# Pairing each 64-slot expert with a 128-slot expert, block by block, in a two-layer decoder trunk

## The chip, the cores and the metric

The kernel runs on one core of a Trainium2 chip. The metric is device time in microseconds. The kernel before takes 1368.06 us (median of 3 runs, 1367.66 to 1368.17).

## What is computed

256 tokens of width 1024 go through two decoder layers in float32. The part that matters here is the channel mixer of the second layer, eight experts of which each token uses two:

```
logits = xn @ w_router                      # (256, 8)
top_v, top_i = top_k(logits, 2);  gates = softmax(top_v) put at top_i
for e in range(8):
    ye = (silu(xn @ w_gate[e]) * (xn @ w_up[e])) @ w_down[e]    # 1024 -> 3584 -> 1024
    out = out + gates[:, e:e+1] * ye
```

Around it stand an attention layer with its dense mixer, a pooling mixer, norms and a gated per-layer input. They are the same in both kernels.

## The kernel before

**Precision.** Each float32 weight is used as a high part and a low part in a 32-bit matmul type. ScalarE copies the raw weights to `w_hi` (`split_hi`, L297), VectorE subtracts to get `w_lo` (`split_lo`, L314), and TensorE runs three matmuls per product: high by high, low by high, high by low (`product`, L334 to L336).

**Units.** Weights come in units of 128x2048 elements (1 MB), numbered `u` in one sequence over the whole kernel. SP loads them into seven buffers `raw`; a load waits for the `split_lo` of the unit seven before it. `w_hi` and `w_lo` have three buffers each (`SPLIT = 3`): `split_hi(u)` waits until TensorE has used unit u-3 (`unit_used`). Both splits run two units ahead in the order of the code (`AHEAD = 2`).

**Experts.** The tokens of an expert are gathered into 128 slots by a matmul with a 0/1 matrix (`pick`), and the result is scattered back by a matmul with its transpose (`pick_t`). An expert's turn has seven blocks of 512 hidden columns. A block has six units: two of the gate matrix (G1, G2 here), two of the up matrix (U1, U2) and two of the down matrix (D1, D2) for the hidden columns of the block before. Between them ScalarE does the silu (L1386), VectorE the product `hiddens` (L1887), TensorE turns the hidden tile (L865), and ScalarE and VectorE split it again (`hidden_hi`, `hidden_lo`).

**Small experts.** VectorE sorts the experts by their token count (`sort_experts`, `place_experts`, in turn 0). The three with the fewest tokens have 64 slots: their rows are put side by side as high and low part, so that up and down products take two matmuls and not three (`product_few`, L1048 and L1049). Hidden tiles are turned and summed by a matmul with `fold` (L862). Expert 0 runs first while the sort is done, then the three small ones, then four of 128 slots:

```
turn(1, 0, few=True)
turn(2, 0, few=True, few_before=True)
turn(1, 2, few=True, few_before=True)
turn(2, 2, few_before=True)
with pe.Fori(3, pairs + 1) as it:      # one pass, two turns
    ...
turn(1, turns - 1, end=True)
```

**Between turns.** Every second turn gathers the tokens of the two next experts in its last block, in banks 5 and 6 (`gather_pair`). The result of a turn is complete in banks 3 and 4 after the first block of the next; ScalarE and VectorE split it (`result_hi` L1503, `result_lo` L2121), TensorE scatters it in four quarters in the second block, and VectorE adds each, times its gate, to the residual (`add_result`, L2130). TensorE, ScalarE, VectorE and SP each run a list of instructions in the order written in the code, and wait for each other by semaphores.

Of the kernel before, what the change touches and what calls it, by code (L numbers as in the profile page):

```python
# [20 lines left out]
F32 = mybir.dt.float32  # L21
# [46 lines left out]
RANK_AT = (0, 5, 6, 7, 1, 2, 3, 4)  # L68
FEW_AT = (1, 2, 3)


def trunk(nc, dram):
    ctx = ExitStack()
    with ctx:
# [66 lines left out]
        gate_at = sb("gate_at", [P, TT, 2 * NE])  # L141
        place_at = sb("place_at", [P, TT, 2 * NE + 1])
        rank_at = sb("rank_at", [P, NE])
# [3 lines left out]
        order = sb("order", [P, NE], I32)  # L147
# [19 lines left out]
        few_hidden = h_t_hi[:, :].rearrange("p (c h s) -> p c h s", c=4, h=2)  # L167
        sort_cols, sort_area = qk_gain[:, :, :].rearrange("p a d -> p (a d)"), rope[:, :, :, :].rearrange("p t a n -> p (t a n)")
        sort_key, sort_rank, sort_over, sort_count = (sort_cols[:, n * NE:(n + 1) * NE] for n in range(4))
        sort_own = sort_cols[:, DH:DH + NE * NE].rearrange("p (a e) -> p a e", a=NE)  # L170
        sort_work = sort_area.rearrange("p (t a e) -> p t a e", t=TT, a=NE)
# [149 lines left out]
        def load(eng, u, view, k=0):  # L321

            dst = raw_slot(u).rearrange("p (c n) -> p c n", c=view.shape[1])
            if in_wide(u):
                eng.dma_start(dst, view).then_inc(extra_landed[u - U_WIDE], 16)
                return
            if u >= RAW:
                before_it = ring(u) - RAW
                split_wait(eng, before_it if before_it < U_WIDE else before_it + EXTRA, k)
            eng.dma_start(dst, view).then_inc(landed[ring(u) % RAW], 16)  # L330
# [21 lines left out]
        def _(sp):  # L352
# [81 lines left out]
            def expert_units(e, e_before, u, first=False):  # L434

                units = []
                for f in range(FB):
                    views = [expert_rows(w, e, 4 * half, 4, 512 * f, 512) for w in (ge, ue) for half in range(2)]
                    if f or not first:
                        views += [expert_rows(de, e if f else e_before, 4 * ((f - 1) % FB) + 2 * half, 2, 0, D)  # L440
                                  for half in range(2)]
                    units += [(u + n, view) for n, view in enumerate(views)]
                    u += len(views)
                return units

            def load_expert(e, e_before, k):
                for u, view in expert_units(e, e_before, U_TURN):
                    load(sp, u, view, k)


            first_expert = expert_units(0, None, U_MOE, first=True)
# [15 lines left out]
            e_before = 0  # L467
            for at in range(1, NE):
                e = expert_at(slice(at, at + 1))
                load_expert(e, e_before, at - 1)  # L470
                e_before = e
            extra = sp.value_load(more[0:1, 0:1], min_val=0, max_val=NE)
            with sp.If(extra > 0):
                load_expert(0, expert_at(slice(NE - 1, NE)), NE - 1)
                with sp.Fori(1, NE) as it:
                    load_expert(expert_at(bass.ds(it, 1)), expert_at(bass.ds(it - 1, 1)), it + (NE - 1))
            turns = extra + (NE - 1)
            e = expert_at(slice(NE - 1, NE))
            for half in range(2):
                load(sp, U_TURN + half, expert_rows(de, e, 4 * (FB - 1) + 2 * half, 2, 0, D), turns)  # L480
# [40 lines left out]

        def gathered_of(i, e):

            return ps[:, 5 + i % 2, :].rearrange("p (c e s) -> p c e s", c=2, e=2)[:, :, e, :]
# [43 lines left out]
        def _(pe):  # L568
# [441 lines left out]
            def gather_pair(part, t0, k=0):  # L1010

                if part == 0:
                    pe.wait_ge(pick_ready, t0 + 3 + k)
                    if t0:
                        pe.wait_ge(added, 4 * (t0 + k))
                    else:
                        pe.wait_ge(rows_split_lo, 2)
                else:
                    pe.wait_ge(xe_lo_ready, 2 * (t0 + 1 + k) + 2)
                for c in range(4 * part, 4 * part + 4):  # L1020
                    for rows, tt in ((a_hi, 0), (a_hi, 1), (a_lo, 0), (a_lo, 1)):
                        at = (c % 2) * 2 * SLOTS
                        last = nc.tensor.matmul(ps[:, 5 + (c % 4) // 2, at:at + 2 * SLOTS],  # L1023
# [3 lines left out]
                    if c % 2:  # L1027
                        last.then_inc(gathered, 1)

            def scatter(q, t, k=0):  # L1030

                pe.wait_ge(y_lo_ready, t + 1 + k)
                pe.wait_ge(pick_t_copied, t + 1 + k)
                if q < 2 and t % 2 == 0:
                    pe.wait_ge(xe_lo_ready, 2 * (t + 3 + k))
                elif q < 2:
                    pe.wait_ge(added, 4 * (t + k))
                else:
                    pe.wait_ge(added, 4 * (t + k) + q - 1)
                tt, half = q // 2, q % 2  # L1040
                for y, stop in ((y_hi, False), (y_lo, True)):
                    last = nc.tensor.matmul(ps[:, 5 + q % 2, :], pick_t[:, tt * P:(tt + 1) * P],  # L1042
# [8 lines left out]
            def down(u, f, half, g, k=0, end=False, h_t=(h_t_hi, h_t_lo), few=False):  # L1051
# [3 lines left out]
                for n in range(2):  # L1055
                    for c in range(2):
                        at = (2 * half + c) * P
                        first, stop = f == 0 and half == 0 and c == 0, f == FB - 1 and half == 1 and c == 1
                        w = weights(u, c, 512 * n, 512, D)
                        if few:  # L1060
                            last = product_few(ps[:, 3 + n, :], h_t_hi[:, at:at + P], w, first, stop)
                        else:
                            last = product(ps[:, 3 + n, :], (h_t[0][:, at:at + P], h_t[1][:, at:at + P]), w, first, stop)
# [4 lines left out]
            def turn(t0, k=0, end=False, few=False, few_before=False):  # L1068

                x = xb if t0 == 2 else xe  # L1070

                def x_of(c):
                    return x[:, 2 * c * P:(2 * c + 1) * P], x[:, (2 * c + 1) * P:(2 * c + 2) * P]

                for f in range(FB):
                    u, g = turn_unit(t0, f), JF + FB * t0 + f
                    for n, freed in ((0, silu_ready), (1, hidden_ready)):
                        for half in range(2):
                            unit(u, k)
                            if f == 0 and n == 0 and t0 < 2:  # L1080
                                pe.wait_ge(xe_lo_ready, 2 * (t0 + k) + (half + 1) * (t0 + 1))
                            if half == 0:
                                pe.wait_ge(freed, g + FB * k)
                            for c in range(4):
                                d, w = 4 * half + c, weights(u, c, 0, 512, 512)
                                if few and n == 1:
                                    both = x[:, 2 * d * P + FEW:2 * d * P + FEW + P]
                                    last = product_few(ps[:, n, :], both, w, d == 0, d == KD - 1)
                                else:
                                    last = product(ps[:, n, :], x_of(d), w, d == 0, d == KD - 1)  # L1090
                            last.then_inc(unit_used, 1)
                            u += 1
                        if t0 == 0 and f == 1 and n == 0:
                            transpose_hidden(g - 1, k)
                    if f == 1 and t0:
                        scatter(0, t0 - 1, k)
                        scatter(1, t0 - 1, k)
                    if f == 2:
                        if t0:
                            pe.wait_ge(pick_t_copied, t0 + k)  # L1100
                        for tt in range(TT):
                            last = nc.tensor.transpose(ps[:, 7, tt * P:(tt + 1) * P],
                                                       pick_of(t0 // 2, tt).bitcast(F32), ident[:, :])
                        last.then_inc(pick_transposed, 1)
                    if f or t0:
                        if f == 1 and t0:
                            pe.wait_ge(y_lo_ready, t0 + k)
                        for half in range(2):
                            if f == FB - 1 and t0 != 1:
                                gather_pair(half, t0, k)  # L1110
                            down(u, (f - 1) % FB, half, g - 1, k, few=few if f else few_before)
                            if end and f == FB - 1 and half == 0:
                                transpose_hidden(g, k)
                            u += 1
                    if f == 1 and t0:
                        scatter(2, t0 - 1, k)
                        scatter(3, t0 - 1, k)
                    if (f or t0) and not (end and f == FB - 1):
                        transpose_hidden(g, k, few)
# [3 lines left out]
            turn(0)  # L1123
            pe.wait_ge(more_ready, 1)
            extra = pe.value_load(more[0:1, 0:1], min_val=0, max_val=NE)
            turns = extra + (NE - 1)
            pairs = pe.value_load(more[0:1, 1:2], min_val=0, max_val=NE // 2) + (NE // 2 - 1)
# [1270 lines left out]
```

## Time and profile before

| quantity | value |
|---|---|
| median of 3 runs | 1368.06 us |
| the profiled execution | 1368.13 us |
| its span | 1366.4 us |
| TensorE busy | 1325.6 us, 97% |
| VectorE busy | 1154.0 us, 84% |
| ScalarE busy | 951.8 us, 70% |
| granted TensorE clock, all slices | full |
| bytes read from HBM | 420.27 MB |

The shares are over the whole span. Matmuls are pipelined: the profile gives each a length of 0.39 us, while one starts every 0.23 us, so that a TensorE share near 100% still can hold short waits. The seven turns after the first take the stretch from 492 to 1322 us.

### The profile page before, as it was taken

To read this page: it belongs to the slowest core of one execution; us is meant where nothing else is said; L and a number is where in the kernel's file an instruction comes from. 1 tells how busy PE (TensorE), PEld (TensorE's weight loads), DVE (VectorE), ACT (ScalarE), POOL (GpSimd) and SP (SyncE) were. 2 spreads that over 40 slices of the span, in tenths; PEclk is the share of its full clock that TensorE was granted. 3 is DMA by queue.
4 is the path that set the end of the run, shared out by engine and by line. 5 is a ranking of instruction groups with operands and counts; after the bars stand their busy time and mean duration, and the time that the engine had idled before them with its cause. 6 is when DMAs were issued, how large, how long until landed. Compare 5 with 4: busy or idle time off the path is not lost.

```text
span 1366.4 us, 17261 instructions
## 1 busy us (share of the span) xinstructions
PE 1325.6 (97%) x6404; PEld 1082.8 (79%) x6404; DVE 1154.0 (84%) x970; ACT 951.8 (70%) x874; POOL 71.5 (5%) x110
## 2 busy tenths in 40 slices
PE   8999999999999999999999999999999999999998
PEld 7776888888877887777777777888888888888887
DVE  6897655556889989999999999998898899889886
ACT  5676544446777777777777777777777777776775
POOL 2120910000200000000000000000000000000000
PEclk9999999999999999999999999999999999999999
DMA  8743765555299889999999999999999999999980
GB/s 305 266 130 89 256 203 195 185 185 162 86 357 347 317 323 359 393 395 393 394 393 390 380 394 395 394 372 371 337 351 375 377 349 359 376 337 359 358 329 31
DMA packets 197860, 422.46 MB, mean 309 GB/s; under 512 B 13064, under 2 KB 37392, under 8 KB 197776
## 3 DMA queue, kind: packets, MB, share of 16 engines
q1 hardware_dynamic: 197776, 421.35, 85.2%
q8 instruction: 52, 0.85, 0.3%
q14 instruction: 32, 0.26, 0.0%
HBM read 420.27 MB, written 1.05 MB: 308 GB/s over the span
## 4 chain that ended last, share of the span: by engine, by line
PE 74%; DVE 16%; ACT 5%; issue 3%; SPq 1%; DMA 1%; POOL 0%; ACTq 0%; DVEq 0%; POOLq 0%
PE ps L334 19%; PE ps L336 19%; PE ps L335 19%; DVE w_lo L314 12%; PE ps L885 5%; ACT w_hi L297 4%; PE ps L883 3%; PE ps L1048 1%; PE ps L865 1%; PE ps L1023 1%; PE ps L1049 1%; PE ps L862 1%; PE ps L882 1%; DMA raw<-in_attn_w_qkv_dram 1%; PE ps L1042 1%
## 5 line engine op out<-in xcount | busy, mean ns | idle before, releaser
L314 DVE TENSOR_TENSOR w_lo<-raw,w_hi 128x2048 fp32r<-128x2048 f32 x382 | 867.8, 2290 | 128.6 <-ACT w_hi L297 127.4
L297 ACT ACTIVATE w_hi<-raw 128x2048 fp32r<-128x2048 f32 x385 | 732.6, 1914 | 122.2 <-PE ps L336 100.0
L334 PE MATMUL ps<-w_hi,xe 128*128 128x512 f32 x448 | 178.4, 398 | 3.0 <-DVE w_lo L314 2.9
L336 PE MATMUL ps<-w_hi,xe 128*128 128x512 f32 x448 | 174.8, 390 | 0.0
L335 PE MATMUL ps<-w_lo,xe 128*128 128x512 f32 x448 | 174.5, 390 | 0.0
L334 PE MATMUL ps<-w_hi,h_t_hi 128*128 128x512 f32 x360 | 141.4, 393 | 0.5 <-DVE w_lo L314 0.5
L336 PE MATMUL ps<-w_hi,h_t_lo 128*128 128x512 f32 x360 | 140.3, 390 | 0.0
L335 PE MATMUL ps<-w_lo,h_t_hi 128*128 128x512 f32 x360 | 140.2, 389 | 0.0
L334 PE MATMUL ps<-w_hi,xb 128*128 128x512 f32 x280 | 111.4, 398 | 1.9 <-DVE w_lo L314 1.9
L885 PE MATMUL ps<-a_all,w_hi 128*128 128x512 f32 x308 | 109.8, 396 | 0.0
L336 PE MATMUL ps<-w_hi,xb 128*128 128x512 f32 x280 | 109.2, 390 | 0.0
L335 PE MATMUL ps<-w_lo,xb 128*128 128x512 f32 x280 | 109.1, 390 | 0.0
L334 PEld LDWEIGHTS ps<-w_hi,xe 128*128 128x128 f32 x448 | 84.1, 188 | 21.7 <-DVE w_lo L314 5.3
L336 PEld LDWEIGHTS ps<-w_hi,xe 128*128 128x128 f32 x448 | 84.1, 188 | 18.1
L335 PEld LDWEIGHTS ps<-w_lo,xe 128*128 128x128 f32 x448 | 84.2, 188 | 16.4
L883 PE MATMUL ps<-a_all,w_lo 128*128 128x256 f32 x352 | 90.9, 279 | 0.0
L2286 POOL TENSOR_TENSOR rstd<-mean_sq,minus_half 128x1 f32<-128x1 f32 (+2 forms) x20 | 23.9, 1199 | 1267.2 <-DVE mean_sq L1588 1186.0
L334 PE MATMUL ps<-w_hi,a_all 128*128 128x512 f32 (+1 forms) x216 | 84.5, 391 | 0.1
L1048 PE MATMUL ps<-w_hi,h_t_hi 128*128 128x512 f32 x168 | 69.8, 415 | 14.8 <-DVE w_lo L314 13.4
L336 PE MATMUL ps<-w_hi,a_all 128*128 128x512 f32 (+1 forms) x216 | 81.9, 379 | 0.0
L335 PE MATMUL ps<-w_lo,a_all 128*128 128x512 f32 (+1 forms) x216 | 81.6, 378 | 0.0
L334 PEld LDWEIGHTS ps<-w_hi,h_t_hi 128*128 128x128 f32 x360 | 67.6, 188 | 15.6 <-DVE w_lo L314 2.4
(319 smaller groups left out, 1856.9 us busy)
## 6 DMA issues: line engine op xcount, KB each, us to landing
raw<-in_moe_w_gate_dram SPq DMA_DIRECT2D x112, 1024.0 KB, 7.6
raw<-in_moe_w_up_dram SPq DMA_DIRECT2D x111, 1024.0 KB, 7.4
raw<-in_moe_w_down_dram SPq DMA_DIRECT2D x111, 1024.0 KB, 7.4
raw<-in_attn_w_qkv_dram SPq DMA_DIRECT2D x11, 1024.0 KB, 12.6
raw<-in_ffn_w_gate_dram SPq DMA_DIRECT2D x11, 1024.0 KB, 5.3
raw<-in_ffn_w_up_dram SPq DMA_DIRECT2D x11, 1024.0 KB, 5.3
raw<-in_ffn_w_down_dram SPq DMA_DIRECT2D x11, 1024.0 KB, 5.0
raw<-in_ple_w_gate_dram SPq DMA_DIRECT2D x8, 1024.0 KB, 6.9
```

Source lines behind the costliest of these rows:

```text
L297: nc.scalar.activation(w_hi[:, u % SPLIT, :], raw_slot(u), ACT.Copy).then_inc(hi_ready, 1)
L314: nc.vector.tensor_tensor(w_lo[:, u % SPLIT, :], raw_slot(u), w_hi[:, u % SPLIT, :].bitcast(F32), ALU.subtract).then_inc(lo_ready, 1)
L334: nc.tensor.matmul(out, x[0], w[0], start=first, stop=False)
L335: nc.tensor.matmul(out, x[0], w[1], start=False, stop=False)
L336: return nc.tensor.matmul(out, x[1], w[0], start=False, stop=last)
L862: last = nc.tensor.matmul(ps[:, 2, n * FEW:(n + 1) * FEW], hidden[:, n * P:(n + 1) * P], fold[:, :], start=True, stop=True)
L865: last = nc.tensor.transpose(ps[:, 2, n * P:(n + 1) * P], hidden[:, n * P:(n + 1) * P], ident[:, :])
L882: nc.tensor.matmul(ps[:, bank, :], w[0], a_all[:, :, cols], start=True, stop=False)
L883: last = nc.tensor.matmul(ps[:, bank, 0:SEQ], w[1], a_hi[:, cols], start=False, stop=False)
L885: last = nc.tensor.matmul(ps[:, bank, :], w[0], a_all[:, :, cols], start=False, stop=c == KD - 1)
L1048: nc.tensor.matmul(out, x, w[0], start=first, stop=False)
L2286: return nc.gpsimd.tensor_tensor(rstd[:, at:at + n], mean_sq[:, at:at + n], minus_half[:, 0:n], ALU.pow)
```

## The change

The order of the experts by token count becomes (0, 5, 1, 6, 2, 7, 3, 4), so that after expert 0 there are three pairs of a small and a large expert, and one large expert last. A pair runs its 14 blocks alternately: a block of the small one, a block of the large one, and so on. The down units of a block belong to the block of the same expert, two blocks before. Each of the two has its own pair of result banks, `Y_BANKS` (3 and 4, 6 and 7). Scatter and turned picks share bank 5; the gather uses banks 5 and 2. The small hidden tile has its own buffer (`few_t`), and the picks of both experts are turned together and copied by ScalarE instead of VectorE. The hidden tile of one block is turned after the first gate unit of the next. The silu moves behind the third `split_hi` of a block, and `hiddens` behind the fifth `split_lo`. The places of the experts in the sort grow from 8 to 19 (`PLACES`), for turns that only run when an expert has more tokens than slots. `SPLIT`, `RAW` and `AHEAD` stay.

```diff
-RANK_AT = (0, 5, 6, 7, 1, 2, 3, 4)
+RANK_AT = (0, 5, 1, 6, 2, 7, 3, 4)
+PLACES = NE + len(SECOND)
...
+        few_t = p_t_hi[:, 0, :]
+        picks_t = p_t_lo[:, 0, :]
+        Y_BANKS = (6, 3)
...
+        PAIR_BLOCKS = [(f, e) for f in range(FB) for e in range(2)]
+        SCATTERS = {(0, 1, 1): (-1, 0), (0, 1, 3): (-1, 1), (0, 1, 5): (-1, 2), (1, 0, 1): (-1, 3),
+                    (1, 0, 5): (0, 0), (1, 1, 1): (0, 1), (1, 1, 3): (0, 2), (1, 1, 5): (0, 3)}
...
+            def pair(k, first=False):          # TensorE
+                for f, e in PAIR_BLOCKS:
+                    few, x, g = e == 0, (xe, xb)[e], block_at_seq(f, e)
...
+                    for n in range(2):
+                        for half in range(2):
...
+                            gate_or_up(u + 2 * n + half, n, half, x, g, k, few)
+                            if n == 0 and half == 0:
...
+                                transpose_hidden(g - 1, k, few=e == 1)
+                            if f == 3 and e == 0 and n == 1 and half == 0:
+                                transpose_picks(k, 2)
+                            if f == FB - 1 and e == 1 and n == 1:
+                                gather_piece(half, k + 2, g + FB * k)
+                            between(2 * n + half)
...
+                    down(u + 4, f_down, 0, g_down, t_down, k, few=few)
...
+                    down(u + 5, f_down, 1, g_down, t_down, k, few=few)
+                    between(5)
...
+            def pair(k, first=False):          # ScalarE
+                for f, e in PAIR_BLOCKS:
+                    g, u = block_at_seq(f, e), pair_unit(f, e, first)
+                    for n in range(4 if first and f == 0 and e == 0 else 6):
+                        split_hi(u + n + AHEAD, k)
+                        if f == 0 and e == 1 and n == 0 and not first:
+                            result_hi(u - 1, -1, k)
+                        if f == 1 and e == 0 and n == 2:
+                            result_hi(u - 1, 0, k, free=not first)
+                        if n == 1:
+                            hidden_hi(g - 1, k, few=e == 1)
+                        if n == 2:
+                            silus(g, u + 1, k)
...
+            def pair(k, slots, first=False):   # VectorE
+                for f, e in PAIR_BLOCKS:
...
+                        split_lo(u + n + AHEAD, k)
+                        if f == 0 and e == 1 and n == 0 and not first:
+                            result_lo(-1, k)
+                        if f == 1 and e == 0 and n == 2:
+                            result_lo(0, k)
+                        if n == 1:
+                            hidden_lo(g - 1, k, few=e == 1)
+                        if n == (3 if bare else 4):
+                            hiddens(g, u + 3, k)
...
+                        if f == 4 and e == 0 and n == 3:
+                            picks(4, 1, k, iota_slot[:, :])
...
-                    then(nc.vector.tensor_tensor(sort_work, a[:, :, :].unsqueeze(2).to_broadcast([P, TT, NE, NE]),
-                                                 sort_own.unsqueeze(1).to_broadcast([P, TT, NE, NE]), ALU.mult))
+                    then(nc.vector.tensor_tensor(sort_work, a[:, :, :].unsqueeze(2).to_broadcast([P, TT, PLACES, NE]),
+                                                 sort_own.unsqueeze(1).to_broadcast([P, TT, PLACES, NE]), ALU.mult))
...
-            turn(1, 0, few=True)
-            turn(2, 0, few=True, few_before=True)
-            turn(1, 2, few=True, few_before=True)
-            turn(2, 2, few_before=True)
+            pair(0, first=True)
+            pair(2)
             with pe.Fori(3, pairs + 1) as it:
-                turn(1, (it - 1) * 2)
-                turn(2, (it - 1) * 2)
-            turn(1, turns - 1, end=True)
+                pair((it - 1) * 2)
+            last_turn(turns - 1)
```

## Rows read from the trace of the kernel before

**Rows 1.** Busy time by engine in stretches of time: small block, large block, turns, whole stretch.
```profile
core 0: us, PE busy (x) PEld busy (x) DVE busy (x) ACT busy (x) POOL busy (x), PEclk, DMA share, GB/s
578.26:593.82 15.56, 14.43 (x65) 11.23 (x64) 14.34 (x9) 12.04 (x8) 0.00 (x0) 1.00 1.04 394
936.44:953.23 16.79, 16.79 (x85) 14.18 (x84) 14.86 (x10) 11.61 (x10) 0.00 (x0) 1.00 1.03 379
720.70:835.06 114.36, 106.34 (x477) 82.33 (x475) 107.00 (x71) 87.91 (x62) 0.00 (x0) 1.00 1.04 389
1077.30:1197.63 120.33, 120.07 (x551) 99.20 (x550) 108.08 (x67) 87.31 (x59) 0.00 (x0) 1.00 1.00 365
492.46:1321.71 829.25, 807.50 (x3665) 651.30 (x3665) 756.26 (x480) 619.86 (x431) 0.00 (x0) 1.00 1.00 371
```

**Rows 2.** Who waited for whom, small block 578.26 to 593.82 (total, times, longest).
```profile
PEld ps L1048 <- DVE w_lo L314: 2.3, 3, 1.5
DVE w_lo L314 <- ACT w_hi L297: 1.2, 2, 0.9
```

**Rows 3.** VectorE in order of time, small block (start, length, instruction, idle before).
```profile
583.61 2.29 DVE L314 TENSOR_TENSOR w_lo<-raw,w_hi 128x2048 fp32r<-128x2048 f32 x1
586.27 2.29 DVE L314 TENSOR_TENSOR w_lo<-raw,w_hi 128x2048 fp32r<-128x2048 f32 x1 [0.37 <-ACT w_hi L297]
589.41 4.49 DVE L314 TENSOR_TENSOR w_lo<-raw,w_hi 128x2048 fp32r<-128x2048 f32 x2 [0.85 <-ACT w_hi L297]
593.82 0.68 DVE L1887 TENSOR_TENSOR tmp<-tmp,ps 128x512 f32<-128x512 f32 x1
594.42 4.49 DVE L314 TENSOR_TENSOR w_lo<-raw,w_hi 128x2048 fp32r<-128x2048 f32 x2
```

**Rows 4.** ScalarE in order of time, the same block.
```profile
586.97 0.60 ACT L1386 ACTIVATE tmp<-ps 128x512 f32<-128x512 f32 x1 [0.74 <-PE ps L336]
587.47 5.51 ACT L297 ACTIVATE w_hi<-raw 128x2048 fp32r<-128x2048 f32 x3
```

**Rows 5.** TensorE in order of time, the same block: the first matmul of each part.
```profile
581.20 0.50 PE L334 MATMUL ps<-w_hi,xe 128*128 128x512 f32 x1
...
586.77 0.39 PE L1048 MATMUL ps<-w_hi,xe 128*128 128x512 f32 x1
...
588.62 0.50 PE L1048 MATMUL ps<-w_hi,xe 128*128 128x512 f32 x1
...
591.76 0.50 PE L1048 MATMUL ps<-w_hi,h_t_hi 128*128 128x512 f32 x1 [1.04 <-DVE w_lo L314]
...
593.96 0.50 PE L1048 MATMUL ps<-w_hi,h_t_hi 128*128 128x512 f32 x1
...
595.93 1.00 PE L862 MATMUL ps<-fold,tmp 128*128 128x64 f32 x8
596.76 0.50 PE L334 MATMUL ps<-w_hi,xe 128*128 128x512 f32 x1
```

**Rows 6.** TensorE in order of time, between two large blocks.
```profile
923.37 0.60 PE L865 MATMUL ps<-ident,tmp 128*128 128x128 f32 x4
923.72 0.48 PE L334 MATMUL ps<-w_hi,xb 128*128 128x512 f32 x1
```

**Rows 7.** Groups of instructions by line, 492.46 to 1321.71 (busy, mean ns, idle before).
```profile
L2130 DVE SCALAR_TENSOR_TENSOR resid<-ps,gate_at,resid 128x512 f32<-128x512 f32 x28 | 19.6, 743 | 0.0
L2121 DVE TENSOR_TENSOR y_lo<-ps,y_hi 128x1024 fp32r<-128x1024 f32 x7 | 8.5, 1217 | 0.3 <-ACT y_hi L1503 0.3
L1503 ACT ACTIVATE y_hi<-ps 128x1024 fp32r<-128x1024 f32 x7 | 7.2, 1022 | 0.0
```

**Rows 8.** VectorE and TensorE in order of time, sort and placing in turn 0.
```profile
405.14 0.22 DVE L2076 TENSOR_TENSOR rope<-qk_gain 128x64 f32<-128x64 f32 x1
...
421.23 0.28 DVE L2094 TENSOR_TENSOR rope<-place,qk_gain 128x128 f32<-128x128 f32 x1
...
410.81 0.50 PE L334 MATMUL ps<-w_hi,xe 128*128 128x512 f32 x1 [1.55 <-DVE w_lo L314]
...
425.16 0.50 PE L334 MATMUL ps<-w_hi,h_t_hi 128*128 128x512 f32 x1 [0.18 <-DVE w_lo L314]
```

More of the change, by code:

```diff
@@ L1066, in down, with gate_or_up @@
                 last.then_inc(unit_used, 1)
[L1068 to L1073, printed above, removed]
+            def gate_or_up(u, n, half, x, g, k=0, few=False):
+                unit(u, k)
+                if half == 0:
+                    pe.wait_ge((silu_ready, hidden_ready)[n], g + FB * k)
+                for c in range(4):
+                    d, w = 4 * half + c, weights(u, c, 0, 512, 512)
+                    if few and n == 1:
+                        both = x[:, 2 * d * P + FEW:2 * d * P + FEW + P]
+                        last = product_few(ps[:, n, :], both, w, d == 0, d == KD - 1)
+                    else:
+                        rows = x[:, 2 * d * P:(2 * d + 1) * P], x[:, (2 * d + 1) * P:(2 * d + 2) * P]
+                        last = product(ps[:, n, :], rows, w, d == 0, d == KD - 1)
+                last.then_inc(unit_used, 1)
@@ L1075, in turn, with transpose_picks, first_turn @@
+            def transpose_picks(k, experts):
+                pe.wait_ge(added, 4 + 4 * k)
+                for e in range(experts):
+                    for tt in range(TT):
+                        at = (e * TT + tt) * P
+                        last = nc.tensor.transpose(ps[:, 5, at:at + P], pick_of(e, tt).bitcast(F32), ident[:, :])
+                last.then_inc(pick_transposed, experts)
+            def first_turn():
                 for f in range(FB):
-                    u, g = turn_unit(t0, f), JF + FB * t0 + f
@@ L1077, in turn @@
-                    for n, freed in ((0, silu_ready), (1, hidden_ready)):
+                    u, g = turn_unit(0, f), JF + f
+                    gather = f == FB - 1
+                    for n in range(2):
                         for half in range(2):
[L1079 to L1094, printed above, removed]
@@ L1115, in turn @@
[L1115 to L1119, printed above, removed]
+                    if f:
+                        down(u + 4, f - 1, 0, g - 1, 0)
+                        if gather:
+                            gather_piece(2, 0, g)
+                            gather_piece(3, 0, g)
+                        down(u + 5, f - 1, 1, g - 1, 0)
+                        if not gather:
+                            transpose_hidden(g)
@@ new lines, in piece_hi, with result_hi @@
+            def piece_hi(i, k):
+                act.wait_ge(gathered, 3 + i + 2 * k)
+                for e, x in enumerate((xe_parts, xb_parts)):
+                    last = nc.scalar.activation(x[:, 2 * i:2 * i + 2, 0, :], gathered_of(i, e), ACT.Copy)
+                last.then_inc(xe_hi_ready, 1)
+            def result_hi(u, t, k=0, free=True):
+                used(u, k)
+                if free:
+                    act.wait_ge(scattered, 4 * t + 4 * k)
+                nc.scalar.activation(y_hi[:, :].rearrange("p (b n) -> p b n", b=2), y_of(t), ACT.Copy).then_inc(y_hi_ready, 1)
@@ new lines, in last_turn @@
+            def last_turn(k):
+                for f in range(FB):
+                    g, u = JF + FB + f, last_unit(f)
+                    for n in range(6 if f else 8):
+                        split_hi(u + n + AHEAD, k)
+                        if f == 0 and n == 6:
+                            result_hi(u + 5, -1, k)
+                        if f == 2 and n == 2:
+                            result_hi(last_unit(0) + 7, 0, k)
+                        if n == 1:
+                            hidden_hi(g - 1, k)
+                        if n == 2:
+                            silus(g, u + 1, k)
+                        if f == 4 and n == 3:
+                            act.wait_ge(scattered, 4 + 4 * k)
+                            copy_picks(2 + k, slice(0, TT * P), 1)
+                        if f == FB - 1 and n == 4:
+                            hidden_hi(g, k, to=a_hi[:, 0:512])
@@ L1534, in _ @@
                 nc.scalar.activation(a_hi[:, tt * D:(tt + 1) * D], xs[:, tt, :], ACT.Copy).then_inc(rows_split_hi, 1)
-            turn(0)
+            first_turn()
             act.wait_ge(more_ready, 1)
-            extra = act.value_load(more[0:1, 0:1], min_val=0, max_val=NE)
+            extra = act.value_load(more[0:1, 0:1], min_val=0, max_val=EXTRA_TURNS)
             turns = extra + (NE - 1)
-            pairs = act.value_load(more[0:1, 1:2], min_val=0, max_val=NE // 2) + (NE // 2 - 1)
-            turn(1, 0, few=True)
-            turn(2, 0, few=True)
-            turn(1, 2, few=True)
-            turn(2, 2)
+            pairs = act.value_load(more[0:1, 1:2], min_val=0, max_val=EXTRA_TURNS // 2) + 3
+            pair(0, first=True)
+            pair(2)
             with act.Fori(3, pairs + 1) as it:
-                turn(1, (it - 1) * 2)
-                turn(2, (it - 1) * 2)
-            turn(1, turns - 1, end=True)
+                pair((it - 1) * 2)
+            last_turn(turns - 1)
             split_hi(U_TURN + AHEAD, turns)
@@ L2203, in _ @@
-            turn(0, few_next=(True, True))
+                    u, g = turn_unit(0, f), JF + f
+                    for n in range(0 if f else 1, 4):
+                        split_lo(u + n + AHEAD)
+                        if f == 1 and n == 1:
+                            hidden_lo(g - 1)
+                        if f == 1 and n == 3:
+                            sort_experts()
+                        if f == 2 and n == 2:
+                            place_experts()
+                        if f in (3, 4) and n == 2:
+                            rows_lo_of(f - 3)
@@ new lines, in last_turn @@
+            def last_turn(k):
+                for f in range(FB):
+                    g, u = JF + FB + f, last_unit(f)
+                    for n in range(6 if f else 8):
+                        split_lo(u + n + AHEAD, k)
+                        if f == 0 and n == 6:
+                            result_lo(-1, k)
+                        if f == 2 and n == 2:
+                            result_lo(0, k)
+                        if n == 1:
+                            hidden_lo(g - 1, k)
+                        if n == (3 if f == FB - 1 else 4):
+                            hiddens(g, u + 3, k)
+                        if (f, n) in LAST_SCATTERS:
+                            t, q = LAST_SCATTERS[f, n]
+                            add_result(q, t, k)
+                        if f == FB - 1 and n == 4:
+                            hidden_lo(g, k, to=(a_hi[:, 0:512], a_lo[:, 0:512]))
@@ L2204, in _ @@
+            first_turn()
             dve.wait_ge(more_ready, 1)
[L2205 removed]
+            extra = dve.value_load(more[0:1, 0:1], min_val=0, max_val=EXTRA_TURNS)
             turns = extra + (NE - 1)
[L2207 to L2211 removed]
+            pairs = dve.value_load(more[0:1, 1:2], min_val=0, max_val=EXTRA_TURNS // 2) + 3
@@ L2212, in _ @@
+            pair(0, iota_few[:, :], first=True)
+            pair(2, iota_few[:, :])
             with dve.Fori(3, pairs + 1) as it:
-                turn(1, (it - 1) * 2)
-                turn(2, (it - 1) * 2)
-            turn(1, turns - 1, end=True)
+                pair((it - 1) * 2, iota_next)
+            last_turn(turns - 1)
             split_lo(U_TURN + AHEAD, turns)
```

462 lines of the change are left out of this document (274 added, 188 removed).

## The prediction

> **What bounds the kernel now.** I read the stretches of time first, block by block, because the share of TensorE over the whole span says only that it is rarely idle. The turns of the experts take 829.25 us of the span. A block of a large expert takes 16.79 us with TensorE busy all the time and VectorE 14.86. A block of a small expert takes 15.56, with TensorE at 14.43 and VectorE at 14.34 [rows 1]. So large blocks are bound by TensorE, and small ones by something that neither engine's busy time shows.
>
> The waits of a small block name it: TensorE waits for `w_lo` three times, and VectorE waits for `w_hi` twice in the same block [rows 2]. The order of time shows the loop. TensorE starts U1 at 586.77, when G2 is done. Only then may ScalarE split D1, which takes G2's buffer. It does the silu first at 586.97, then D1's high part at 587.47; VectorE follows at 589.41, after an idle 0.85, and TensorE starts D1 at 591.76 [rows 3 to 5]. From there VectorE runs without a gap: D1, D2, `hiddens`, and the next G1 from 594.42, which TensorE takes up at 596.76.
>
> What is lost: from U1 to the next G1 are 9.99 us [rows 5]. Work in it is 4 short units of 8 matmuls. A matmul starts every 0.2265 us: from 581.20 to 586.77 there are 24, the first of them 0.11 longer after its wait (5.57 = 24 x 0.2265 + 0.13) [rows 5]. That makes 7.25, and fold takes 596.76 - 595.93 = 0.83. So 9.99 - 8.08 = 1.91 us are lost in each of 21 small blocks, 40 us in all. That is all that interleaving could win.
>
> **The steady pair of blocks.** TensorE's work is unchanged: the same matmuls, turns and folds in another order. The question is whether the 1.91 goes. A split buffer is free only when TensorE is done with the unit three before. At the end of G2 of a small block VectorE has already waited 0.37 and 0.85 for it [rows 3], so the buffers were full, and TensorE was two units behind them. A large block ahead can't make them fuller: VectorE's spare time there is spent waiting for a free buffer. Four short units follow as before. I therefore walk the new order with the same distances, counted from U1's start:
> - ScalarE begins D1's high part at +0.20 (586.97 - 586.77), as the silu now stands behind it. VectorE starts 1.94 later (589.41 - 587.47), at +2.14, and TensorE 2.35 after that (591.76 - 589.41), at +4.49. Before it was +4.99 [rows 3 to 5].
> - D1's high part takes a further 1.83 in a run (5.51 for three), then the silu 0.50, so D2's high part starts at +2.53 and VectorE at +4.47. It was free at +4.34 (splits in a run are 2.20 apart, 4.49 - 2.29) [rows 3, 4]. TensorE has D2 at +6.82.
> - The next unit is G1 of the large block. `hiddens` no longer stands ahead of it, so VectorE begins at +6.67 and TensorE has it at +9.02.
>
> Work in this stretch is 7.25 alone, since fold has moved into the large block. Lost: 9.02 - 7.25 = 1.77. So silu and `hiddens`, 0.50 and 0.60, leave the chain, but fold's 0.83 no longer covers it.
>
> The pair then is: small block 5.44 for the gate, 0.49 for turning the large hidden tile (a large block's 16.79 less 72 x 0.2265 = 16.31; the turns themselves fill 0.35 of it [rows 1, 6]), and 9.02, together 14.95. Large block: 16.31 + 0.83 + 0.11 for the start after a wait + 0.11 after the fold = 17.36. Sum 32.31, against 15.56 + 16.79 = 32.35 now. Over 21 pairs of blocks: -1 us. Bounds: -40 if no wait is left, and +8 if both gate starts and D2 slip by a further 0.2 each (21 x 0.4).
>
> **Between turns.** The same four gathers, 28 scatters and 16 turned picks. A small turn costs 114.36 against 7 x 15.56 = 108.92 [rows 1], 5.4 with its gather, part of it in time that was lost anyway. A large one without a gather costs 120.33 - 7 x 16.79 = 2.8. In a pair, the small expert's block 1 has `result_hi` between D1 and the silu and `result_lo` between D1 and D2. The chain gets later by VectorE's 1.22 less its wait of 0.13, so some 1.0; two scatter quarters of 2 x 0.2265 = 0.45 in the same block cover 0.9 of it. The `picks` ahead of a G1 cost at most 0.35 (the nearest row, a VectorE pass of 128 elements, takes 0.28 [rows 8]). The other results fall into large blocks with spare time. I take +0.5 for three pairs. Bounds: nothing to gain beyond the -1.8 of one scatter set hidden in lost time, and +11 from the rival below [rows 7].
>
> **Sort and placing.** They stand in VectorE's queue in turn 0, where TensorE already waits for `w_lo` behind them: 1.55 at 410.81, and 0.18 at 425.16 [rows 8]. So every longer instruction counts in full. An operation on 64 elements takes 0.22 and one on 128 takes 0.28, about 0.001 per element. Four placing operations go from 128 to 304 elements: 4 x 0.18 = 0.7. Three sort operations go from 64 to 152: 0.3. New are a compare, two operations for `iota_next` and a wait that was not there, less one copy: 0.2 + 0.6 + 0.1 - 0.2 = 0.7. Together +1.7; bounds 0 (the large block absorbs it in its spare 1.9, 16.79 - 14.86 [rows 1]) and +3. The memsets added on GpSimd come long before anyone waits and cost nothing. The copy of the picks, now on ScalarE, lies in a large block once and once in D2's stretch, after the low split of D1: nothing.
>
> **Transfers.** Small turns move 394 GB/s now, and no wait for a landing shows on ScalarE [rows 1, 2]. Interleaved, 12 MB-units take 32.3 us, 12 x 1.0486 / 32.3 = 390 GB/s. It was hidden at the higher rate, so it stays hidden; without that cover the wait would fall on ScalarE ahead of each high split.
>
> **The sum.** -1.0 + 0.5 + 1.7 = +1.2 us on the profiled execution's 1368.13, hence 1369.3; this execution stands 0.07 above the median, so 1369.2 for the median.
>
> The trace has the two regimes that the Trainium skill's page Perfetto Trace Analysis (Optimization Strategy) speaks of: where the most-contended engine changes over time, interleaving the regimes may help. By that rule the wait would go and the time would be near 1330; it is rival A. The same section says that a gap repeating on the engine that should be saturated can mean too few buffers for the next tile. The gap before D1 repeats in each small block, and by this second rule interleaving alone leaves it. The chain of rows 3 to 5 bears out the second.
>
> **Rivals.**
> - A. Interleaving evens the load out in full: VectorE goes into a small block far enough ahead. For it: averaged over two blocks, VectorE needs 29.2 and TensorE 30.5 of 32.35. Against it: three split buffers. Price -40 + 0.5 + 1.7, hence 1330. Chance 5%.
> - B. Only the first wait stays, 4.49 - 3.63 = 0.86, and D2 and the next G1 come without one, because ScalarE and VectorE have shorter queues there than I count. It saves (1.77 - 0.86) x 21 = 19 us more: 1350. Chance 12%.
> - C. Slower: the between-turn work of a pair lands one for one in the short stretch of a small block, since nothing is spare there. Place: block 1 of the small expert and the blocks of `picks`. Price per pair: 1.02 + 1.22 + 2 x 0.74 + 0.35 = 4.1 [rows 7], 12 over three, less the 0.5 counted: 1381. It decides once ScalarE waits for `scattered` or VectorE for a scatter ahead of D1 or D2, as bank 5 now serves all four quarters in turn. Chance 12%.
> - D. The pairs don't run as described, because more tokens than slots ask for extra turns. The rooms by rank are the same, so this would show in both. Chance under 1%.
>
> **How the numbers follow.** My forecast has 70%, with some 2.5 us to both sides. The time of this kernel can be told from no change beyond about 0.2%, 2.7 us: below 1365.3 is faster, above 1370.8 slower. Faster: A and B 0.17, and 0.06 of the forecast's share, together 0.22. Slower: C 0.12 and a quarter of the forecast's share, 0.29. Same: 0.49. The range 1360 to 1376 holds the forecast with some slip in the D chain on both sides (0.2 to 0.4 per small block is 4 to 8 us), and leaves out A, B and most of C.
>
> **What would show it.** In a pair, one `hiddens` to the second next should be 32.3 apart. TensorE should wait for `w_lo` at D1 (0.9), D2 (0.4) and at G1 of the large block (0.3), and nowhere in the large block. ScalarE's idle time before the high split should be released by TensorE in both kinds of block. The wait at 410.81 should grow by 0.5 and that at 425.16 by 1.2. I am wrong if the wait before D1 is gone, or if TensorE waits inside large blocks.

## The result

The changed kernel takes 1371.39 us (median of 13 runs, 1369.88 to 1373.38), the kernel before 1368.21 us (13 runs, 1367.66 to 1370.13). The ratio is 1.0019, with a 95% interval of 1.0011 to 1.0028: some 2.6 us slower, at the edge of what can be told from no change. 1369.2 had been forecast, in a range of 1360 to 1376.

The profiled execution of the changed kernel has a span of 1368.6 us against 1366.4. TensorE executes 6404 matmuls in both and is busy 97% of both spans. Nearly all of the difference stands in one place. Turn 0, from its first product of the hidden tile to its last, goes from 99.21 to 101.08. The 49 blocks after it go from 829.25 [rows 1] to 829.46. What comes before and after is the same within 0.2.

Stretches of time of the changed kernel (columns as in rows 1): a small block, the large block after it, all 49 blocks, and turn 0.
```profile
661.49:677.35 15.86, 14.92 (x66) 11.39 (x64) 14.77 (x10) 12.72 (x9) 0.00 (x0) 1.00 1.03 381
677.35:693.87 16.52, 16.43 (x77) 13.69 (x77) 14.49 (x9) 11.78 (x8) 0.00 (x0) 1.00 1.02 380
494.47:1323.93 829.46, 804.74 (x3666) 650.64 (x3665) 756.52 (x472) 619.60 (x435) 0.00 (x0) 1.00 1.01 373
393.39:494.47 101.08, 97.28 (x442) 78.96 (x441) 92.30 (x76) 70.22 (x49) 0.00 (x0) 1.00 0.94 340
```
The same turn of the kernel before:
```profile
393.25:492.46 99.21, 97.25 (x442) 78.95 (x441) 90.89 (x75) 70.03 (x48) 0.00 (x0) 1.00 0.97 347
```
A pair of blocks takes 15.86 + 16.52 = 32.38, where one of each took 15.56 + 16.79 = 32.35 [rows 1]. VectorE is busy 1.4 us longer in turn 0, and TensorE as long as before: its wait grew.

TensorE in order of time in one small block of a pair: the first matmul of U1, D1, D2 and of G1 of the large block. They answer to rows 5.
```profile
668.44 0.39 PE L1111 MATMUL ps<-w_hi,xe 128*128 128x512 f32 x1
...
673.00 0.50 PE L1111 MATMUL ps<-w_hi,p_t_hi 128*128 128x512 f32 x1 [0.77 <-DVE w_lo L324]
...
675.28 0.50 PE L1111 MATMUL ps<-w_hi,p_t_hi 128*128 128x512 f32 x1 [0.17 <-DVE w_lo L324]
...
677.49 0.50 PE L344 MATMUL ps<-w_hi,xb 128*128 128x512 f32 x1
```
Counted from U1's start, D1 comes at 4.56, D2 at 6.84 and G1 at 9.05. The walk had 4.49, 6.82 and 9.02. All three delays are there, though the profile marks only two of them as waits (0.77 and 0.17): eight matmuls take 1.81, and G1 comes 2.21 after D2, so 0.4 late. TensorE is busy 16.43 of the large block's 16.52.

### The profile page after: what moved, and what is told of

It reads as the page before. It is cut to its first block, busy times and chain, and to the rows that moved or that the text cites. A ratio compares the mean times of both kernels' runs of the same rounds, so it can differ in the third digit from the quotient of the medians.

```text
span 1368.6 us, 17326 instructions
## 1 busy us (share of the span) xinstructions
PE 1323.0 (97%) x6404; PEld 1082.3 (79%) x6404; DVE 1155.5 (84%) x963; ACT 951.6 (70%) x879; POOL 72.3 (5%) x133
## 4 chain that ended last, share of the span: by engine, by line
PE 76%; DVE 15%; ACT 5%; issue 2%; SPq 1%; DMA 1%; POOL 0%; ACTq 0%; DVEq 0%; POOLq 0%
PE ps L344 20%; PE ps L346 19%; PE ps L345 19%; DVE w_lo L324 11%; PE ps L952 5%; ACT w_hi L307 4%; PE ps L950 3%; PE ps L929 1%; PE ps L1092 1%; PE ps L932 1%; PE ps L1105 1%; PE ps L949 1%; PE ps L1111 1%; DMA raw<-in_attn_w_qkv_dram 1%; PE ps L1112 1%
## 5 line engine op out<-in xcount | busy, mean ns | idle before, releaser
L344 PE MATMUL ps<-w_hi,xe 128*128 128x512 f32 x392 | 156.3, 399 | 1.7 <-DVE w_lo L324 1.5
L346 PE MATMUL ps<-w_hi,xe 128*128 128x512 f32 x392 | 153.1, 391 | 0.0
L345 PE MATMUL ps<-w_lo,xe 128*128 128x512 f32 x392 | 152.8, 390 | 0.0
L344 PE MATMUL ps<-w_hi,h_t_hi 128*128 128x512 f32 x360 | 141.0, 392 | 2.2 <-DVE w_lo L324 2.2
L344 PE MATMUL ps<-w_hi,xb 128*128 128x512 f32 x336 | 135.2, 402 | 4.1 <-DVE w_lo L324 3.5
L346 PE MATMUL ps<-w_hi,xb 128*128 128x512 f32 x336 | 131.3, 391 | 0.0
L345 PE MATMUL ps<-w_lo,xb 128*128 128x512 f32 x336 | 131.0, 390 | 0.0
L1111 PE MATMUL ps<-w_hi,p_t_hi 128*128 128x512 f32 x168 | 70.3, 418 | 20.0 <-DVE w_lo L324 19.1
L344 PEld LDWEIGHTS ps<-w_hi,xe 128*128 128x128 f32 x392 | 73.7, 188 | 16.7 <-DVE w_lo L324 2.6
L346 PEld LDWEIGHTS ps<-w_hi,xe 128*128 128x128 f32 x392 | 73.6, 188 | 15.9
L345 PEld LDWEIGHTS ps<-w_lo,xe 128*128 128x128 f32 x392 | 73.8, 188 | 14.3
L344 PEld LDWEIGHTS ps<-w_hi,xb 128*128 128x128 f32 x336 | 63.1, 188 | 23.7 <-DVE w_lo L324 7.8
```

Of the source, the lines that this page charges most:

```text
L344: nc.tensor.matmul(out, x[0], w[0], start=first, stop=False)
L345: nc.tensor.matmul(out, x[0], w[1], start=False, stop=False)
L346: return nc.tensor.matmul(out, x[1], w[0], start=False, stop=last)
L1111: nc.tensor.matmul(out, x, w[0], start=first, stop=False)
```

## The experiments

Each is compared with the kernel before on the same chip.

| kernel | median us | ratio to before, 95% | one small + one large block |
|---|---|---|---|
| turns (before) | 1368.2 | 1 | 15.56 + 16.79 |
| pairs (the change) | 1371.39 | 1.0019 (1.0011 to 1.0028) | 32.38 |
| pairs, silu and `hiddens` at old places | 1389.81 | 1.0153 (1.0137 to 1.0168) | 33.29 |
| pairs, short sort | 1368.58 | 1.0001 (0.9992 to 1.0010) | 32.38 |
| turns, silu late | 1361.49 | 0.9953 (0.9936 to 0.9970) | 15.22 + 16.79 |
| turns, four buffers | 1368.68 | 1.0001 (0.9992 to 1.0010) | 15.56 + 16.79 |
| turns, four buffers, silu late | 1361.68 | 0.9947 (0.9932 to 0.9962) | 14.17 once, later 15.9, + 16.79 |
| the same, half the down bytes | 1344.57 | 0.9826 (0.9810 to 0.9843) | 14.16 + 16.79 |
| pairs, four buffers | 1334.48 | 0.9752 (0.9737 to 0.9767) | 14.14 + 16.47 |
| pairs, fourth buffer for high parts alone | 1336.29 | 0.9762 (0.9747 to 0.9777) | 14.57 + 16.05 |
| pairs, four buffers, half the down bytes | 1333.82 | 0.9748 (0.9733 to 0.9763) | 14.15 + 16.51 |
| pairs, four buffers, short sort | 1334.10 | 0.9746 (0.9733 to 0.9759) | 14.14 + 16.47 |

### Pairs with four split buffers

From the first pair on the split buffers form a ring of four; the fourth ones lie where `xs` and `extra_raw` were.

```diff
+        def slot(u, k):
...
+            return (u - U_TURN) % 4
...
+        def hi_slot(u, k=0):
...
+            at = slot(u, k)
+            return hi_fourth[:, :] if at == 3 else w_hi[:, at, :]
...
+        def lo_slot(u, k=0):
...
+            at = slot(u, k)
+            return lo_fourth[:, :] if at == 3 else w_lo[:, at, :]
...
-                nc.scalar.wait_ge(unit_used, u - SPLIT + 1 + PER_EXPERT * k)
+                nc.scalar.wait_ge(unit_used, u - depth(u, k) + 1 + PER_EXPERT * k)
```

> The changed kernel with a fourth buffer for the high and for the low parts from the first pair on (a split waits for the unit four before, not three; the order of every queue stays). Theory (the three split buffers hold the wait): D1's high part no longer waits for the end of G2, the waits before D1, D2 and the next G1 go, and a pair of blocks falls from 32.4 us to the TensorE work of about 30.6, 21 times: 1333 to 1338 us. If the transfers bind then (12 units in 30.6 us are 411 GB/s, above the 394 of the small turns), it ends later, 1338 to 1350. Rival (ScalarE and VectorE are too slow in the four short units whatever the buffers): within 3 us of 1371.

1334.48 us, 37 less than the three-buffer pairs. A pair of blocks takes 14.14 + 16.47 = 30.61; TensorE's work alone is 32.35 - 1.91 = 30.44 by the numbers of the kernel before. The whole answer to who waited for whom in most of a small block (575.5 to 588):
```profile
ACT p_t_hi L1559 <- PE ps L960: 1.2, 1, 1.2
ACT hi_fourth L337 <- PE ps L376: 0.8, 1, 0.8
ACT tmp L1554 <- PE ps L376: 0.6, 1, 0.6
ACT w_hi L337 <- PE ps L376: 0.4, 1, 0.4
```
TensorE and VectorE are in no line: neither waits. All that is left is ScalarE waiting for TensorE. Over the whole block one wait of 0.2 us of TensorE's weight load for `w_lo` is added. VectorE is busy from end to end of this block, and so is TensorE by the profile; its row, with the large one after it:
```profile
574.59:588.73 14.14, 14.14 (x68) 11.73 (x67) 14.14 (x10) 11.10 (x8) 0.00 (x0) 1.00 1.04 391
588.73:605.20 16.47, 16.47 (x78) 13.67 (x77) 14.85 (x10) 13.34 (x11) 0.00 (x0) 1.00 1.04 395
```
The three buffers held the wait.

### Turns with four split buffers

The same edit in the kernel before.

> The kernel before with the same fourth buffers from turn 1 on. Theory: here the silu stands ahead of D1's high part in ScalarE's queue and itself waits for the end of G2, so that the fourth buffer is of no use to D1, and small blocks stay at 15.5 to 15.6 us: 1367 to 1369 us. Rival (the fourth buffer alone is what counts, pairs or not): 10 to 40 us faster.

1368.68 us, and small blocks at 15.56. ScalarE in order of time there:
```profile
599.84 1.90 ACT L327 ACTIVATE hi_fourth<-raw 128x2048 fp32r<-128x2048 f32 x1
603.34 0.60 ACT L1419 ACTIVATE tmp<-ps 128x512 f32<-128x512 f32 x1 [1.59 <-PE ps L366]
603.84 5.51 ACT L327 ACTIVATE w_hi<-raw 128x2048 fp32r<-128x2048 f32 x3
```
The silu waits 1.59 us for the end of G2, and D1's high part stands behind it in the queue, though its buffer is free. So a deeper ring needs the silu out of its way in ScalarE's queue.

### Pairs with the silu and `hiddens` at their old places

```diff
+                        if n == 2:
+                            silus(g, u + 1, k)
                         split_hi(u + n + AHEAD, k)
...
-                        if n == 2:
-                            silus(g, u + 1, k)
...
-                        if n == (3 if bare else 4):
+                        if n == 3:
                             hiddens(g, u + 3, k)
```

> The changed kernel with the silu again ahead of the third high split of a block, and the product of the hidden tile again ahead of the next block's first low split. Theory (the walk along the chain): D1 gets 0.50 later, the next G1 another 0.6, so that 2.7 us are lost per small block instead of 1.8: 20 us slower than the changed kernel, 1389 to 1393, a pair of blocks at 33.3. Rival (the chain is held by TensorE's release of buffers alone): within 3 us of 1371.

1389.81 us, a pair of blocks at 33.29. Counted from U1's start, D1 comes at 4.98, D2 at 7.18 and G1 at 9.98, nearly where the kernel before had D1 and G1 (4.99 and 9.99). The silu moves D1 by 0.42 and the product adds 0.59 between D2 and G1, against 0.50 and 0.60 in the walk, so both are on the chain. In the changed kernel their new places pay for what fold no longer covers.

### Turns with the silu late

```diff
-                    silus(g, u + 1, k)
                     split_hi(u + 2 + AHEAD, k)
+                    silus(g, u + 1, k)
                     split_hi(u + 3 + AHEAD, k)
```

> The kernel before with one change, the silu behind the third high split of a block; three split buffers. Theory (the walk): D1 comes 0.50 earlier in each small block and D2 at most 0.13 later than VectorE allows, so that 0.3 to 0.5 of the 1.91 us goes: small blocks at 15.05 to 15.25, 6 to 10 us faster, 1358 to 1362. Rival (VectorE's run from D1 to the next G1 starts later for another reason): 1368.

1361.49 us, small blocks at 15.22 instead of 15.56. One line moved is worth 6.4 us to the kernel before by the ratio. In the profiled execution turn 0, which has the line too, went to 97.2, 2.0 less, and the 49 blocks got 5.0 shorter. The steady small blocks, 0.34 each, promise 7.1. Transfers are the likely reason for the rest, though no run tests it: ScalarE waits 7.7 us for landings in these blocks, where it waited for none before.

### Pairs with the sort on 8 places

```diff
-                    then(nc.vector.tensor_tensor(sort_work, a[:, :, :].unsqueeze(2).to_broadcast([P, TT, PLACES, NE]),
-                                                 sort_own.unsqueeze(1).to_broadcast([P, TT, PLACES, NE]), ALU.mult))
+                    then(nc.vector.tensor_tensor(sort_work[:, :, 0:NE], a[:, :, :].unsqueeze(2).to_broadcast([P, TT, NE, NE]),
+                                                 sort_own[:, 0:NE].unsqueeze(1).to_broadcast([P, TT, NE, NE]), ALU.mult))
...
-                pair((it - 1) * 2, iota_next)
+                pair((it - 1) * 2, iota_slot[:, :])
```

The sort itself is cut in the same way, and the subtraction of `base_at` and the two operations for `iota_next` are left out.

> The changed kernel with the sort and the placing on 8 places as before, not 19, and without the two operations that choose the slots of later pairs (turns that only an overfull expert needs are left unprepared). Theory: the 1.9 us that turn 0 got longer come from these operations, and all of them go: 1.5 to 2 us faster than the changed kernel, the stretch from the first to the seventh product of turn 0 back to 99.2 us. Rival (turn 0 is longer because of the copies of the picks on ScalarE or the gather in pieces): under 0.5 us.

1368.58 us, level with the kernel before, and 0.18% below the change by the two ratios. VectorE's part of it, the placing and the low split behind it, in the changed kernel:
```profile
421.86 0.47 DVE L2276 TENSOR_TENSOR tmp<-place,tmp 128x304 f32<-128x304 f32 x1
...
424.83 2.29 DVE L324 TENSOR_TENSOR w_lo<-raw,w_hi 128x2048 fp32r<-128x2048 f32 x1
```
and in the short one:
```profile
422.45 0.28 DVE L2277 TENSOR_TENSOR tmp<-place,tmp 128x128 f32<-128x128 f32 x1
...
423.74 2.29 DVE L324 TENSOR_TENSOR w_lo<-raw,w_hi 128x2048 fp32r<-128x2048 f32 x1
```
Placing takes 424.83 - 421.86 = 2.97 in one and 1.29 in the other, 1.68 less. Yet the profiled turn 0 fell only from 101.08 to 100.70, not to the 99.2 expected. The row of the stretch right behind the sort says why, first in the changed kernel, then in the short one:
```profile
410.50:414.50 4.00, 3.05 (x13) 2.55 (x14) 4.00 (x4) 1.84 (x2) 0.00 (x0) 1.00 0.58 188
```
```profile
410.50:414.50 4.00, 4.00 (x11) 3.15 (x12) 4.00 (x3) 0.85 (x1) 0.00 (x0) 0.57 0.80 254
```
In that execution the granted clock fell to near the lower of its two levels (1.2 of 2.4 GHz) after TensorE's two waits of turn 0. From 410.83 to 413.82 matmuls started 0.43 apart and not 0.23, and nine of them took 3.75 us instead of 2.17, 1.6 more. The same fall stands in the trace of the turns with four buffers, whose turn 0 has the code of the kernel before; it takes 100.78 there, where the kernel before took 99.21:
```profile
392.48:493.26 100.78, 98.86 (x442) 80.08 (x441) 90.87 (x75) 69.99 (x48) 0.00 (x0) 0.98 0.95 342
```
The mean granted clock of most executions is on record, so the two causes can be told apart. Of the changed kernel's 13 executions, the six at a mean clock of 1.000 took 1369.88 to 1370.64 and the seven at 0.998 or 0.999 took 1371.39 to 1373.38. For the kernel before, 37 executions beside the experiments have it: 26 at 1.000 with a median of 1368.14 and none above 1368.68, and 11 below 1.000 with a median of 1369.60. At 1.000 the changed kernel stands at 1370.28, and with the short sort at 1368.27 (six of 11 executions). So the longer sort costs 2.0 us, in every execution, as expected, and the fall of the clock 1.5 in some.

### Four buffers and silu late, turns one after the other

Both edits above in the kernel before.

> The kernel before (turns one after the other) with the fourth split buffers and the silu moved behind D1's high part, as the pairs have it. It asks what the interleaving itself is worth once D1 need not wait. Theory: a small block is then bound by VectorE's 6 x 2.20 + 0.60 + 0.34 = 14.1 us, large blocks stay at 16.8 by TensorE: small blocks from 15.56 to 14.2 to 14.5, in all 1345 to 1350 us. The pairs with four buffers, at 1334.5, would then owe 10 to 15 us to the interleaving. Rival (buffers and the silu's place do it all, interleaving nothing): as fast as the pairs with four buffers, 1334 to 1337.

1361.68 us: missed, 12 us above the band. One early small block did take 14.17, but the next took 15.28 and later ones 15.9. Two of them:
```profile
559.57:573.74 14.17, 14.07 (x65) 11.32 (x64) 14.17 (x9) 10.62 (x8) 0.00 (x0) 1.00 1.04 394
620.86:636.75 15.89, 15.11 (x67) 11.99 (x68) 15.44 (x10) 13.13 (x10) 0.00 (x0) 1.00 1.04 393
```
and the two longest of ScalarE's waits in the second:
```profile
ACT w_hi L327 <- DMA raw<-in_moe_w_gate_dram: 2.4, 3, 0.8
...
ACT w_hi L327 <- DMA raw<-in_moe_w_down_dram: 0.8, 2, 0.6
```
ScalarE waits for landings, which it did nowhere in the 49 blocks of the kernel before. TensorE's weight loads wait 2.4 us for low parts behind it. A block reads 6 x 1.0486 = 6.29 MB; at 394 GB/s that is 15.97 us. The steady small blocks of the kernel before, at 15.56 us, asked for 404 GB/s, already above this rate, but a small turn as a whole (44.0 MB in 114.36 us) only for 385. Here the first blocks outrun the transfers, as far as the seven raw buffers carry, and then the transfers set the pace. The 49 blocks take 824.3, no less than with the silu late alone: what the fourth buffer frees, the transfers take.

### The same with half of the bytes of the down units

```diff
+            if u >= U_TURN and view.shape[1] == 2:
+                dst, view = dst[:, :, 0:512], view[:, :, 0:512]
             eng.dma_start(dst, view).then_inc(landed[ring(u) % RAW], 16)
```

> Turns one after the other, fourth split buffers, silu late, and half of the bytes of each down unit loaded from turn 1 on (the output isn't the reference's). In the run with all bytes, small blocks began at 14.17 us and then went to 15.9, with 394 GB/s flat and ScalarE waiting for landings. Theory (394 GB/s is what transfers give, 6.29 MB then take 15.95 us, and interleaving wins by spreading the bytes over the large blocks): small blocks stay at 14.2, about 17 of them times 1.75, 1330 to 1337 us, level with the pairs. Rival (VectorE's or TensorE's own work keeps them there): 1355 to 1362.

1344.57 us: steady small blocks stay at 14.16, 17 us less in all. That is the transfers' share, and no wait for a landing is left. The forecast of 1330 to 1337 was missed by 8 us. It counted 17 stretched blocks of 1.75 us. Block by block, twelve small blocks got shorter, eight of them by 1.7 us or more, 18.2 us in all. The kernel stays ten us above the pairs, which transfers don't explain.

### Pairs with four buffers: three more

> Pairs with four split buffers, with half of the bytes of each down unit loaded from the first pair on (the second half of the columns is left from an earlier unit, so the output isn't the reference's). It asks whether transfers bind the pairs with four buffers, where ScalarE waited some 27 us for landings. Theory (transfers take a part of the steady time, mostly at the ends of a stretch without boundary work): 2 to 6 us faster than 1334.5, and no waits for landings. Rival (those waits are ahead of need): within 1 us of 1334.5.

1333.82 us, 0.7 less than with all bytes. The waits for landings are gone, but the 2 to 6 us are not gained: those waits lay ahead of need, as the rival has it, and transfers hardly bind the pairs. They are close to it, though: with all bytes the 49 blocks move 391 GB/s on average.

> Pairs with a fourth buffer for the high parts alone; the low parts keep three, and VectorE itself waits for the unit three before. It asks whether the whole chain or only its ScalarE part must start early. Theory: with the high part ready, VectorE can begin D1 at 0.2 us after the end of G2 and TensorE has it at 2.6, a us ahead of its need at 3.6: within 1.5 us of the 1334.5 of both buffers. Rival (VectorE needs the buffer as much): 1345 or more.

```diff
+            if depth(u, k) == 4:
+                nc.vector.wait_ge(unit_used, u - SPLIT + 1 + PER_EXPERT * k)
...
         def lo_slot(u, k=0):
-            at = slot(u, k)
-            return lo_fourth[:, :] if at == 3 else w_lo[:, at, :]
+            return w_lo[:, u % SPLIT, :]
```
1336.29 us, 1.8 above both buffers and so 0.3 outside the band, with intervals that overlap. Nearly all of the gain needs 8 KB per partition, for the high part.

> Pairs with four split buffers and the sort on 8 places: the two findings together. Theory: turn 0 gives back its 1.9 us in full: 1332.5 to 1333. Rival (the stretch after it is now bound by transfers at 394 GB/s, which go on through turn 0 as well, so that the time won is spent waiting for a landing): 1334 to 1334.5.

1334.10 us. The intervals of this and of the long sort overlap, and the clock fell behind the sort in its profiled execution too (0.64 from 410.5 to 414.5). The transfers didn't take the time back there: ScalarE waits for no landing in turn 0, and the 49 blocks take 792.5 against 792.4 with the long sort. The one execution at a mean clock of 1.000 took 1332.75, inside the forecast, and the four at 0.999 took 1334.09 to 1334.48. That speaks for the clock and against the rival, on a single execution. Of the kernels that load all bytes this one is the fastest, by a margin too small to tell from the next.

## Why the prediction was right

- **No gain from interleaving with three buffers: right.** The steady pair was forecast at 32.31 against 32.35 and measured at 32.38. Each of the three steps of the chain came within 0.07. The fourth buffer shows that the ring was the cause, and the old places show that silu and `hiddens` have nearly the cost the walk gave them (0.42 and 0.59 against 0.50 and 0.60).
- **Between turns: right in size, in part by luck.** -1.0 + 0.5 were forecast for the 49 blocks and +0.2 was measured. The steady pairs gave +0.6 (21 x 0.03) and not -1.0, the work between turns -0.4 and not +0.5; the two errors have opposite signs.
- **Sort and placing: right, +1.7 forecast, +1.87 in turn 0.** 0.5 and 1.2 were expected at two waits. The end of the first came 0.5 later against the start of turn 0 (411.45 - 393.39 against 410.81 - 393.25), the second grew by 1.38, from 0.18 to 1.56 [rows 8]. Only the place of the 0.5 was wrong: the wait ahead of the turned hidden tile grew by it, and the one named stayed at 1.54.
- **Transfers: right, but for the margin.** No landing is waited for at the 389 GB/s of a pair (12 x 1.0486 MB in 32.38 us). I took 394 GB/s as a rate that had been reached with ease; it was in fact the most that the transfers give here, as the kernels without the wait show. That it did no harm is luck: the margin was 5 GB/s.
- **The size of the whole.** The profiled executions differ by 2.2, the ratio says 2.6 (1.5 to 3.8), 1.2 was forecast. At a mean granted clock of 1.000 the kernels stand at 1370.28 and 1368.14, 2.1 apart: the sort's 2.0, and next to nothing for the rest. What the medians show beyond it is the clock, which was below 1.000 in seven of the 13 executions of the changed kernel and in 11 of 37 of the kernel before. The sum had no term for it. Whether the change makes the fall more frequent can't be told from so few.
- **Rivals.** A, full levelling, failed with three buffers. With four it came about: 1334, where 1330 had been worked out for it. B failed, as all three delays of the chain stayed. C failed too: the work between turns cost 0.4 less than before and not 12 more.

The Trainium skill's page Perfetto Trace Analysis (Optimization Strategy) has both halves: interleaving regimes whose most-contended engine differs may help, and a gap that repeats can mean too few buffers. The traces agree with both, in this order: first the buffers, then the interleaving. A pair of blocks took 32.38 with three buffers against 32.35 without pairs, and 30.61 with four.

How much is the interleaving worth, once nothing holds it? With four buffers and the silu late, turns take 1361.68 and pairs 1334.48, so 27 us. In the 49 blocks it is more, 824.3 against 792.4, so 32; turn 0 gives back 3.9, since its silu stayed at the old place in the pairs and its sort is longer. With half of the down bytes the 49 blocks take 806.1 and 791.6. So some 17 of the 32 are transfers spread evenly, and 14.5 remain. Steady blocks account for 6 of them (14.16 + 16.79 against 14.15 + 16.51, 21 times), where VectorE's and TensorE's load is levelled; the rest lies where the two orders differ at the ends of turns, and no run takes it apart.

## What to carry to other kernels

When two engines take turns as the bound, interleaving their stages helps only as far as the buffers between them let the one run ahead; if the shared ring is full before the short stretch begins, the same wait comes back. Follow one buffer through its release, each instruction queued ahead of its refill, and its use; that chain, walked with measured distances, gave the time here to 0.1 us per pair of blocks. A queue in program order can undo a deeper ring, and a deeper ring may only uncover the next limit, so test the three (depth, order, bytes) one by one.

## What the runs showed that was not expected

- **Transfers have a flat ceiling of 394 GB/s here.** In the pairs with four buffers they stand at 393 to 395 GB/s in 19 of 20 slices of 33 us in a row, with packets of 2.1 KB on average. Where nothing else holds the small blocks, they take 15.9 us for their 6.29 MB, and 14.16 once a part of the bytes is left out.
- **The granted TensorE clock fell in the middle of a run, in some executions.** Over 410.5 to 414.5 it was 0.57 in the pairs with the short sort, right after waits of 0.30 and 1.54 us (by the profile) between which TensorE did four short transposes. It was 1.00 in the changed kernel, after 0.58 and 1.54. So the waits alone don't decide it, and what does is not shown. A fall costs some 1.6 us, nearly as much as the whole change to the sort.
